# A hybrid attention and mLSTM step: fewer VectorE steps, a normaliser in strips, keys' rotation partners copied by ScalarE

## The reference

```python
aq = partial_rope(rms_norm(aq, q_norm_w), pos)          # 8 heads of 128
ak = partial_rope(rms_norm(ak, k_norm_w), pos)          # returned too, as k_prompt, k_sample
# partial_rope: x1, x2 = xf[..., :16], xf[..., 16:32]
#   concat([x1*cos - x2*sin, x2*cos + x1*sin, xf[..., 32:]])
# attention: softmax(q k^T * scale) v, causal for the prompt;
#   samples: top 3 of 4 blocks of 256 cached keys, by q . mean(keys), then softmax over them
# mLSTM, 4 heads of 256: decayed products q k^T, states C (256 x 256) and normalisers n (256)
n_new = a_prev * n_prev + einsum('bhs,bhsd->bhd', a_s, k)
den   = w_inter * (q . n_prev) + sum(s);  h = num / max(|den|, exp(-m))
y = x + (sigmoid(ga) * (attn*silu(az)) @ w_att + sigmoid(gm) * (h*silu(mz)) @ w_ml) @ w_out
```

## Time and profile before

| | us |
|---|---|
| median of 3 runs | 473.07 (472.76 to 473.12) |
| the profiled execution, its own time | 472.86 |
| its span, first to last instruction | 470.7 |
| PE busy in the span | 458.8 (97%) |
| DVE busy | 402.6 (86%) |
| ACT busy | 289.5 (61%) |

### The profile page before, as it was taken

How to read it: one execution, slowest core, us unless ns; L and a number is a source line. 1 busy time by engine, 2 the same in 40 slices (tenths; PEclk the granted TensorE clock), 3 DMA queues, 4 the chain that set the end, 5 groups by cost and what they waited for, 6 DMA issues and landing times.

```text
span 470.7 us, 11313 instructions
## 1 busy us (share of the span) xinstructions
PE 458.8 (97%) x3823; PEld 417.4 (89%) x3823; DVE 402.6 (86%) x1646; ACT 289.5 (61%) x486; POOL 99.8 (21%) x181
## 2 busy tenths in 40 slices
PE   7999999999989999989999999999999999999997
PEld 5899899898779898878899889899899898899997
DVE  4898899699999997999999999889999874667861
ACT  4866545676973685995485695657848357324430
POOL 2040421013323322422321342312223110000000
PEclk9999999999999999999999999999999999999999
DMA  8899599659999999999999999998999995457511
GB/s 302 321 360 406 179 369 325 226 168 350 297 415 407 411 347 335 394 398 411 408 368 313 404 415 408 410 359 304 378 415 408 410 348 192 141 174 270 179 50 46
DMA packets 44993, 150.89 MB, mean 321 GB/s; under 512 B 6332, under 2 KB 7932, under 8 KB 44808
## 3 DMA queue, kind: packets, MB, share of 16 engines
q1 hardware_dynamic: 20368, 70.77, 41.3%
q0 software_dynamic: 19008, 67.20, 37.2%
q10 hardware_dynamic: 5560, 12.21, 6.7%
HBM read 137.37 MB, written 12.76 MB: 319 GB/s over the span
## 4 chain that ended last, share of the span: by engine, by line
PE 69%; DVE 15%; ACT 8%; issue 4%; DMA 3%; ACTq 0%; POOLq 0%; POOL 0%; DVEq 0%
PE pj L535 26%; PE pj L538 13%; PE wk L535 6%; DVE kpages L1169 4%; PE pa L716 4%; DVE wlo L1070 4%; PE wk L538 3%; DMA kpages<-in_cache_k 3%; DVE cslot L1253 2%; ACT L837 2%; ACT whi L817 2%; PE wk L488 2%; PE wk L640 2%; PE wk L672 1%; PE wk L493 1%
## 5 line engine op out<-in xcount | busy, mean ns | idle before, releaser
L535 PE MATMUL pj<-xn,whi 128*128 128x264 f32 x1328 | 180.6, 288 | 0.8 <-ACT mqT L975 0.7
L535 PEld LDWEIGHTS pj<-xn,whi 128*128 128x128 f32 x1328 | 168.4, 189 | 8.8 <-issue 6.6
L1070 DVE TENSOR_TENSOR wlo<-wraw,whi 128x1024 fp32r<-128x1024 f32 x112 | 137.1, 1228 | 8.7 <-ACT whi L817 8.2
L817 ACT ACTIVATE whi<-wraw 128x1024 fp32r<-128x1024 f32 x112 | 117.9, 1053 | 23.2 <-PE wk L538 13.0
L1169 DVE CUSTOM_DVE_ANT_0 kpages<-kpages,qbc 128x128 f32<-128x128 f32 x512 | 114.9, 288 | 1.7 <-DMA kpages<-in_cache_k 1.6
L538 PE MATMUL pj<-xn,wlo 128*128 128x264 f32 x664 | 94.3, 284 | 3.4 <-DVE wlo L1070 3.4
L538 PEld LDWEIGHTS pj<-xn,wlo 128*128 128x128 f32 x664 | 85.5, 188 | 4.5 <-DVE wlo L1070 4.5
L405 POOL DMA_DIRECT2D kpages<-in_cache_k x64 | 34.3, 536 | 175.2 <-DVE sco L1169 152.2
L405 POOL DMA_DIRECT2D vpages<-in_cache_v x64 | 33.9, 530 | 59.1 <-issue 40.1
L1169 DVE DVE_READ_ACCUMULATOR2_ANT sco<- 128x1 f32 x512 | 41.2, 80 | 0.0
L716 PE MATMUL pa<-vpages,prob 128*32 128x256 f32 x512 | 34.3, 385 | 0.7 <-ACT prob L875 0.7
(11 more groups left out here) (277 smaller groups left out, 634.7 us busy)
## 6 DMA issues: line engine op xcount, KB each, us to landing
wraw<-in_weights SPq DMA_DIRECT2D x112, 512.0 KB, 6.7
kpages<-in_cache_k POOLq DMA_DIRECT2D x64, 512.0 KB, 8.3
vpages<-in_cache_v POOLq DMA_DIRECT2D x64, 512.0 KB, 10.9
cslot<-in_states SPq DMA_DIRECT2D x16, 512.0 KB, 8.6
out_C_s<-cslot ACTq DMA_DIRECT2D x16, 512.0 KB, 8.0
xres<-in_tokens SPq DMA_DIRECT2D x1, 1056.0 KB, 6.8
out_k_p<-kT ACTq DMA_DIRECT2D x4, 256.0 KB, 9.8
out_v_p<-v_nat ACTq DMA_DIRECT2D x4, 256.0 KB, 5.0
```

The costliest lines, as they stand in the source:

```text
L535: mm(bank[:, 0:T], whi[:, q, k, :], src[:, g, k, :], start=(k == 0 and g == 0), stop=False)
L817: A(whi[:, n % WSPLIT], wraw[:, n % WRAW], ACT.Copy).then_inc(whi_ready, 1)
L1070: V.tensor_tensor(wlo[:, n % WRAW], wraw[:, n % WRAW], whi[:, n % WSPLIT], ALU.subtract).then_inc(wlo_ready, 1)
```

## The change

- `ORDER` puts the features of a head of queries or keys in another order, so that the 16 rotated pairs are 32 partitions apart; the weights, norm weights, `rot`, cosines and sines follow it. The host puts the returned keys back in order.
- The keys' partners are no longer made by PE. ScalarE copies partitions 32 to 63 of `kT` to 0 to 31 of a new buffer `swapped`, and 0 to 31 to 32 to 63, at i = 0 and 1 after `split_hi`. VectorE's `rope_norm` reads that buffer, and works on 64 partitions of the keys in its first three steps. The queries' rotation stays on PE.
- `query_rows` does matmuls with a constant `back` (which undoes the order) in place of transposes.
- The prompt's normaliser is made in four strips of 32 output partitions with 64 moving columns each, and stored from four partitions.
- PE no longer waits for `attg_ready` and `mrs_ready` before the keys' sums.
- VectorE: the copy `gmax <- gm` is gone; the scaling of the maxima is folded into the masked maximum; the two mask additions are one instruction; the sample's denominator takes two steps fewer at i = 9, since the query is multiplied with the updated normaliser at i = 6, where the order of steps changes.

```diff
                 def query_rows(bank, first):
...
-                    last = tr(bank[0:NB, (h - first) * P:(h - first + 1) * P], qT[:, h, SEQ:T], P)
+                    last = mm(bank[0:NB, (h - first) * P:(h - first + 1) * P], qT[:, h, SEQ:T], back, start=True, stop=True)
...
-                        pe.wait_ge(attg_ready, 2 * j)
...
-                        pe.wait_ge(mrs_ready, j + 1)
-                    norm_sums(wk[2 * n], wk[2 * n + 1], n, kT[:, n, :])
+                    mm(wk[2 * n][:, 0:T], ones, sq[:, n, :], start=True, stop=True).then_inc(norm_ps, 1)
...
-                    for d in range(EC):
-                        for t in range(2):
-                            col = SEQ - 1 if t == 0 else 383
-                            last = mm(wk[3][:, MHD + d:MHD + d + 1], mk_nat[:, t, d * P:(d + 1) * P], wt[:, col:col + 1],
-                                      start=(t == 0), stop=(t == 1))
+                    part = MHD // VG
+                    for t in range(2):
+                        col = SEQ - 1 if t == 0 else 383
+                        for q in range(VG):
+                            last = mm(wk[3][q * VC:(q + 1) * VC, MHD:MHD + part], wt[:, col:col + 1].broadcast_to([P, VC]),
+                                      mk_nat[:, t, q * part:(q + 1) * part], start=(t == 0), stop=(t == 1))
...
                 split_hi(n + AHEAD)
+                if i < 2:
+                    ch.join()
+                    act.wait_ge(kT_ready, 2 * j)
+                    A(swapped[0:LO, i], kT[LO:2 * LO, i, :], ACT.Copy)
+                    A(swapped[LO:2 * LO, i], kT[0:LO, i, :], ACT.Copy).then_inc(swap_ready, 1)
...
-                    ch.step(V.tensor_copy(gmax[:, b, :], gm[:, b % 2, :]))
...
-                    dve.wait_ge(norm_ps, HEADS + 2 * j + n + 1)
+                    dve.wait_ge(swap_ready, 2 * j + n + 1)
...
-                    V.tensor_scalar(nm[:, n, :], nm[:, n, :], -SCALE, None, ALU.mult).then_inc(smax_ready, 1)
...
-                    ch.step(V.tensor_tensor(wt[:, 0:P], wt[:, 0:P], triT, ALU.add))
-                    V.tensor_tensor(wt[:, SEQ:384], wt[:, P:SEQ], triT, ALU.add).then_inc(wl_ready, 1)
+                    V.tensor_tensor(blocks, wt[:, 0:SEQ].rearrange("p (i t) -> p i t", i=2), triT.unsqueeze(1).broadcast_to([P, 2, P]),
+                                    ALU.add).then_inc(wl_ready, 1)
```

More of the change, by code:

```diff
@@ L188, in build @@
         va = sb("va", [P, 2, 256])
-        nnew = sb("nnew", [P, MH, EC])
+        nnew = sb("nnew", [P, MH, MHD // VG])
         sco = sb("sco", [P, 2, PAGES, HEADS])
@@ L228, in build @@
         mrs = sb("mrs", [P, T])
+        swapped = sb("swapped", [2 * LO, 2, T])
         pj = [ctx.enter_context(nc.psum_tensor(f"pj{i}", [P, 512], F32)) for i in range(2)]
@@ L241, in build @@
         rot = cst[:, C_ROT:C_ROT + P]
+        back = cst[:, C_BACK:C_BACK + P]
         mask3 = cst[:, C_MASK:C_MASK + 384]
@@ L298, in build @@
         xhi_ready, xlo_ready = sem("xhi_ready"), sem("xlo_ready")
+        swap_ready = sem("swap_ready")
         proj, norm_ps, mktr_ps, st_ps, mvtr_ps, g_ps, avtr_ps, den_ps, num_ps = (
@@ L1104, in _, with rope_norm @@
                 split_lo(n)
-            def rope_norm(x, r, ro, done):
-                ch.step(V.tensor_tensor(hT[:, 0, :], ro[:, 0:T], sin, ALU.mult))
-                ch.link(V.tensor_tensor(x, x, cos, ALU.mult))
-                ch.link(V.tensor_tensor(x, x, hT[:, 0, :], ALU.add))
+            def rope_norm(x, r, partners, rows, done):
+                part = slice(0, rows)
+                ch.step(V.tensor_tensor(hT[part, 0, :], partners, sin[part], ALU.mult))
+                ch.link(V.tensor_tensor(x[part], x[part], cos[part], ALU.mult))
+                ch.link(V.tensor_tensor(x[part], x[part], hT[part, 0, :], ALU.add))
                 V.tensor_tensor(x, x, r, ALU.mult).then_inc(done, 1)
@@ L1280, in states_side @@
                     qn, qk = wk[1][:, MHD:MHD + NB], wk[1][:, MHD + NB:MHD + 2 * NB]
[L1281 removed]
+                    w_old, m_exp = bcg[:, 0, j, :], bcg[:, 2, j, :]
                     ch.step(V.tensor_copy(qcs[:, :], wk[1][:, 0:MHD]))
[L1283 to L1284 removed]
+                    ch.step(V.tensor_copy(sst[:, 0], qk))
+                    ch.link(V.tensor_tensor(sst[:, 2], qn, m_exp, ALU.max))
+                    V.scalar_tensor_tensor(out=sst[:, 2], in0=qn, scalar=-1.0, in1=sst[:, 2], op0=ALU.mult, op1=ALU.max).then_inc(qc_read, 1)
                     dve.wait_ge(qc_read, j + 1)
[L1286 to L1288 removed]
                     ch.link(V.reciprocal(sst[:, 2], sst[:, 2]))
@@ L1448, in constants @@
     for m in range(half):
-        c[m + half, C_ROT + m] = -1.0
-        c[m, C_ROT + m + half] = 1.0
+        c[m + LO, C_ROT + m] = 1.0
+        c[m, C_ROT + m + LO] = 1.0
+    c[np.arange(P), C_BACK + ORDER] = 1.0
     r = np.arange(P)
@@ L1477, in weight_chunks @@
 def weight_chunks(w_in, w_proj_mlstm, w_proj_attn, w_out):
-    cuts = [w_in[:, AQ + 256 * n:AQ + 256 * (n + 1)] for n in range(4)]
-    cuts += [w_in[:, g + 256 * j:g + 256 * (j + 1)] for j in range(JOBS) for g in GROUPS]
+    pair = np.concatenate([ORDER, HD + ORDER])
+    cuts = [w_in[:, AQ + 256 * n + pair] for n in range(4)]
+    cuts += [w_in[:, g + 256 * j + (pair if g == AK else np.arange(256))] for j in range(JOBS) for g in GROUPS]
     for w in (w_in[:, GA:GA + D], w_in[:, GM:GM + D], w_proj_mlstm, w_proj_attn, w_out):
@@ L1505 @@
         "consts": constants(),
-        "columns": np.concatenate([cols(n) for n in ("norm_w", "q_norm_w", "k_norm_w", "mh_norm_w")], axis=1),
+        "columns": np.concatenate([cols("norm_w"), cols("q_norm_w")[ORDER], cols("k_norm_w")[ORDER], cols("mh_norm_w")], axis=1),
         "tokens": np.concatenate([np.ascontiguousarray(inputs["x_prompt"])[0], np.ascontiguousarray(inputs["x_sample"])[:, 0]]).T
@@ L1523 @@
     y = g["y"].reshape(P, KC, T).transpose(2, 1, 0).reshape(T, D)
-    k_p = g["k_p"].transpose(3, 0, 2, 1).reshape(rows)
+    there = np.argsort(ORDER)
+    k_p = g["k_p"][:, there].transpose(3, 0, 2, 1).reshape(rows)
     v_p = g["v_p"].reshape(JOBS, P, 2, 256).transpose(2, 1, 0, 3).reshape(rows)
```

55 lines of the change are left out of this document (26 added, 29 removed).

## The result

| | before | changed |
|---|---|---|
| median, us | 473.1 (472.76 to 473.17, 4 runs) | 477.79 (477.75 to 478.44, 4 runs) |
| the profiled execution, its own time | 472.86 | 477.76 |
| its span | 470.7 | 475.6 |
| ratio | | 1.0101, 95% interval 1.0084 to 1.0119 |

The changed kernel is slower by 1.0%, 4.7 us. The forecast was 473.4 with a range to 475.2.

What follows compares the result with a forecast made beforehand. PE was taken to set the pace, with VectorE at the border into job 1 and ScalarE into jobs 2 and 3. 0.9 - 0.9 - 1.4 - 0.2 + 0.8 + 1.3 - 0.2 = +0.3, so 473.4 us, range 471.2 to 475.2.

Steps and rivals of the forecast that it cites:

- sample queries: In query_rows, eight two-pass fp32 matmuls replace eight transposes on PE, which has no wait there: +0.9 us.
- keys' rotation, job 0: Two of eight rotations taken off PE are in job 0, where PE sets the pace: -0.9 us.
- strips: Prompt's normaliser in strips on PE saves 1.1 to 1.8 us over four jobs, where PE has no wait: -1.4.
- job 1 (VectorE's steps, copies): Border into job 1: shorter VectorE steps give -0.2 us; the copies' delay ends in PE's low-weights wait, 0.
- job 2, copies: Border into job 2: four copies bring `mqT` 1.3 us later, PE regains its 0.48 wait before 211.71: +0.8.
- job 3, copies: Border into job 3: the exponential behind `rs` comes 1.3 us later and no following wait takes it up: +1.3.
- clock in jobs 2 and 3: Granted clock stays at 1.00 (2.4 GHz level) in all stretches; nothing in the change should move it: 0.
- last wait: PE's closing 0.4 us wait for the last cached keys shrinks by 0 to 0.4 when PE comes later: -0.2.
- the rival of dear copies: At the borders each ScalarE copy costs its whole 0.42 us, four make 1.7; sum +2.1, median 475.2; chance 0.14.
- The rival of copies that hide: ScalarE has slack at the borders, so copies cost nothing in jobs 2 and 3; median 471.5 us; chance 0.17.
- All that PE saves counts: Rival: all work taken off PE, including all eight key rotations, shortens the time: -4.0 us, median 469.1; chance 0.05.
- The strips did not cost: Rival said normaliser strips cost PE time, two mode changes, 0.2 us a job; sum +2.7, median 475.6; chance 0.05.

Runs made afterwards that it cites:

- filler: Changed kernel plus unused TensorE matmuls inside its waits, four before projection i = 4 of job 2, six before job 3's value pages at i = 3; 474.88 us.
- six_copies: Changed kernel plus two more ScalarE copies of 32 partitions at i = 0 of each job, six a border instead of four; 478.72 us (477.19 to 481.25).

## Why the prediction was wrong

| step | forecast | measured | read from |
|---|---|---|---|
| sample queries | +0.9 | +0.87 | changed, g = 0 to 1 |
| keys' rotation, job 0 | -0.9 | -0.88 | g = 1 to 4 |
| strips | -1.4 | -1.56 | i = 8 to 12 of four jobs: 0.33, 0.35, 0.32, 0.56 |
| job 1 (VectorE's steps, copies) | -0.2 | -0.05 | changed, g = 16 to 22 |
| job 2, copies | +0.8 | +1.16 | filler, g = 32 to 40 |
| job 3, copies | +1.3 | +2.05 | filler, g = 48 to 56 |
| clock in jobs 2 and 3 | 0 | +1.54, +1.55 | changed less filler |
| last wait | -0.2 | about 0 | g = 60 to the end |
| scatter of the start | | +0.3 | g = 0 |
| sum | +0.3 | +5.0 | the two profiled executions differ by 4.9 |

**The step that failed** is the sentence "The granted clock is 1.00 in all of them ..., and nothing here should move it". The same text forecast waits of about 2 and 2.5 us for PE. After 50 us the trace of before has no wait of PE longer than 1.35 us, so it could not say what the clock does behind a longer one, and I took its 1.00 as if it did. That is 3.1 of the 4.7 us. No other step was wrong in kind and cost time: the filler kernel, which is the change without its clock, took 474.9, inside the range and 0.3 under the 475.2 of the rival of dear copies. (That rival's sum leaves out the two terms of -0.2 that the forecast's sum has; with them it is 474.8.)

**The term that was mis-sized** is the copy. I took 0.33, the spacing of an exponential of the same length, between bounds of 0.27 and 0.42. It is 0.44, and the instruction ahead of a pair gives up its overlap: four make 1.9 to 2.0 where 1.3 was put. The upper bound, 1.7 for four, was too low by 0.2 to 0.3, as it left out that a neighbour can lose as well. The Trainium skill ("ScalarE: Activation LUTs", What ACT_TABLE_LOAD costs) gives 186 ns and 0.833 ns a column for an instruction without pointer operands, an estimate of 0.41 for 264 columns, and lets neighbours overlap by some 93 ns. The whole duration agrees (0.42); the overlap does not, since these copies start 0.42 to 0.45 apart even on their own partitions.

**Point by point.**
- What bounds the kernel: right. The loss lies at the borders where the earlier trace rows had ScalarE full, and nowhere else.
- Sample queries, rotation in job 0, strips: right to 0.2 us. In job 0 of the changed kernel the strips begin 0.31 us after two transposes, as L640 did in the earlier trace rows (0.10 late), and the next chunk starts 0.36 after them. That makes 0.46, the lower end of the forecast's 0.45 to 0.64. The old group took 0.82 there (84.84 to 85.66), not the 0.88 of the earlier trace rows: so the saving in jobs 0 to 2, 0.32 to 0.35, lies in the middle of the forecast's 0.24 to 0.43. Job 3's 0.56 lies just above its 0.53:

```profile
84.93 0.38 PE L491 MATMUL wk<-cst,sq 128*8 128x128 f32 x2
85.24 0.43 PE L655 MATMUL wk<-mk_nat,decay 128*32 128x64 f32 x16
85.60 0.63 PE L538 MATMUL pj<-xn,whi 128*128 128x264 f32 x3
```

- Job 1: the time is right by luck, the account is not. The text had PE still wait for VectorE. In fact ScalarE has become the last there too, PE waits 1.71 for `mqT`, and the wait for the low weights is gone. The two waits exchange evenly, so the margin that I named for the dear case (copies of 1.7 passing a wait of 1.35) was already used up: two more copies in six_copies bring the start of i = 4 0.9 later at once, and then the clock falls.
- Job 2: the wait before 211.71 is gone, as forecast, and what PE saved on the rotation counts for nothing. The chain of ScalarE decides, as forecast.
- Job 3: "no wait follows that could take it up" was right.
- The rival of copies that hide fell with PE's waits. "All that PE saves counts" fell too: the 0.9 us of PE's rotations at each of the borders into jobs 2 and 3 came to nothing, as ScalarE's chain ends last there. The strips did not cost; they saved 0.39 a job on average. The Trainium skill ("TensorEngine Tiling (Array Packing)", Instruction Overhead) says that a matmul with one moving column takes as long as one with 60; by that rule the prediction's estimate was a cost of 0.1 a job, and the measurement decides against it.

## What to carry to other kernels

At a place where an engine has no slack, price a new instruction by its whole duration and let its neighbour lose its overlap too; the spacing of another kind of instruction is a lower bound. Where a forecast makes TensorE wait longer than it ever waits in the trace, the clock seen there says nothing about what follows: take a fall with its own price (here 1.5 us each) as a case of the forecast. Work with slack in time, such as partners that are wanted 7 us or more after their issue (the sync engine's DMAs landed 1.9 to 8.6 us after it, and VectorE waited for none), belongs in a DMA from a queue whose engine has nothing to do, not on the engine that is full.

## What the runs showed of the hardware

- Twenty matmul passes that compute nothing made the kernel 2.9 us faster, as they kept the granted clock at 1.00. The Trainium skill ("TensorE: Matmul & The Clock Gate", Part 1) says that an idle TensorE is set back to 1.2 GHz and returns to 2.4 when it works again, and that the number of matmuls at the lower level varies from run to run; the traces agree. Waits of 1.71 and 2.15 us brought a fall in one place and waits of 1.71, 2.31 and 2.14 none in another, so the length of the wait alone does not decide it. After 50 us, no wait of up to 1.64 us brought a fall in any kept trace, and each of the seven waits of 2.57 us or more did. A place with a fall had 3.4 or 6.8 us at the lower level. What decides between 1.7 and 2.3 us was not tried.
- VectorE's addition of 264 columns took 1.27 us in place of 0.42 while GpSimd ran a broadcast of 1.48 us. It ended 0.14 us after the broadcast. With the broadcast moved the stall was gone. The Trainium skill ("SBUF — State Buffer", SBUF: two separate sides) has VectorE with two SBUF inputs and GpSimd take turns at one pair of ports, whole instructions at a time; the trace agrees.
- Four DMA issues in a row on ScalarE, 0.5 to 0.6 us each, left it idle for 1.20 us beyond the 1.07 us of rounding that ran beside them.
